# Twelve unread products behind the spread that ends a stage of a two-layer encoder kernel

## The reference

```python
for l in range(DEPTH):                                   # DEPTH = 2
    h = swiglu_ffn(rms_norm(x, ffn1_norm_pre[l]), ffn1_w_in[l], ffn1_w_out[l])
    x = x + 0.5 * rms_norm(h, ffn1_norm_post[l])
    h = rms_norm(x, mix_norm_pre[l]) @ mix_w_in[l]
    ...                                                  # o_gdn and o_cm from h
    h = jnp.concatenate([o_gdn, o_cm], axis=-1) @ mix_w_out[l]
    x = x + rms_norm(h, mix_norm_post[l])
    h = swiglu_ffn(rms_norm(x, ffn2_norm_pre[l]), ffn2_w_in[l], ffn2_w_out[l])
    x = x + 0.5 * rms_norm(h, ffn2_norm_post[l])
    x = rms_norm(x, block_norm[l])
```

## Time and profile before

| | |
|---|---|
| median of 3 runs | 2207.22 us (2206.28 to 2208.68) |
| the profiled execution's own time | 2205.52 us |
| its span | 2203.8 us |
| TensorE products, busy | 2099.9 us, 95% of the span |
| TensorE weight loads, busy | 1756.1 us, 80% |
| VectorE, ScalarE, GpSimd busy | 1239.1, 682.8 and 38.9 us |
| mean granted TensorE clock | 0.967 of full speed |

### The profile page before, as it was taken

The page is one execution under the profiler, slowest core; times in us unless marked ns, Lnnn a source line. Parts: engine busy times, 40 slices in busy tenths (PEclk is TensorE's granted clock), DMA queues, the critical chain, the costliest instruction groups (busy, mean ns, idle before and its releaser), DMA issues.

```text
span 2203.8 us, 26235 instructions
## 1 busy us (share of the span) xinstructions
PE 2099.9 (95%) x10044; PEld 1756.1 (80%) x10044; DVE 1239.1 (56%) x1707; ACT 682.8 (31%) x914; POOL 38.9 (2%) x51
## 2 busy tenths in 40 slices
PE   7999999997988999999999999999979799999997
PEld 6888887875887788888788888878758778888886
DVE  5555422899855755542375554258988656555323
ACT  5222222434225422222242222233341343222222
POOL 0000000000010000000000000000010000000000
PEclk9999999998999999999999999999979999999997
DMA  5333333223001233333233333323220023333320
GB/s 160 104 95 95 98 95 93 77 77 86 1 1 58 77 99 99 97 87 97 84 96 96 95 93 97 97 67 92 81 58 1 1 67 100 99 97 93 96 79 39
DMA packets 345792, 177.54 MB, mean 81 GB/s; under 512 B 8338, under 2 KB 344692, under 8 KB 345716
## 3 DMA queue, kind: packets, MB, share of 16 engines
q1 hardware_dynamic: 344058, 176.34, 28.0%
q10 hardware_dynamic: 1658, 0.16, 0.1%
HBM read 174.38 MB, written 2.10 MB: 80 GB/s over the span
## 4 chain that ended last, share of the span: by engine, by line
PE 77%; DVE 17%; ACT 3%; issue 2%; DMA 0%; DVEq 0%; SPq 0%; ACTq 0%
PE res L457 21%; PE res L459 21%; PE res L458 21%; DVE u L1301 7%; DVE cacc L1385 2%; PE res L521 1%; PE res L522 1%; PE pq L692 1%; PE stat L464 1%; PE res L525 1%; DVE wl L1137 1%; PE bc L485 1%; DVE pre L1371 1%; PE pq L457 1%; PE pq L459 1%
## 5 line engine op out<-in xcount | busy, mean ns | idle before, releaser
L818 ACT ACTIVATE wh<-raw 128x1024 fp32r<-128x1024 f32 (+1 forms) x336 | 347.8, 1037 | 1014.0 <-PE res L459 993.1
L1137 DVE TENSOR_TENSOR wl<-raw,wh 128x1024 fp32r<-128x1024 f32 (+1 forms) x336 | 401.8, 1197 | 392.6 <-ACT wh L818 392.2
L457 PE MATMUL res<-xh,wh 128*128 128x512 f32 x1576 | 614.2, 390 | 3.0 <-DVE xl L1151 3.0
L458 PE MATMUL res<-xl,wh 128*128 128x512 f32 x1576 | 613.2, 389 | 0.0
L459 PE MATMUL res<-xh,wl 128*128 128x512 f32 x1576 | 613.2, 389 | 0.0
L457 PEld LDWEIGHTS res<-xh,wh 128*128 128x128 f32 x1576 | 295.8, 188 | 65.0 <-DVE wl L1137 2.5
L459 PEld LDWEIGHTS res<-xh,wl 128*128 128x128 f32 x1576 | 295.8, 188 | 61.6
L458 PEld LDWEIGHTS res<-xl,wh 128*128 128x128 f32 x1576 | 295.8, 188 | 61.2
L457 PE MATMUL res<-hh,wh 128*128 128x512 f32 x704 | 273.9, 389 | 0.0
L458 PE MATMUL res<-hl,wh 128*128 128x512 f32 x704 | 273.9, 389 | 0.0
L459 PE MATMUL res<-hh,wl 128*128 128x512 f32 x704 | 273.9, 389 | 0.0
(11 more groups left out here) (268 smaller groups left out, 1936.1 us busy)
## 6 DMA issues: line engine op xcount, KB each, us to landing
raw<-in_ffn_w_in SPq DMA_DIRECT2D x176, 512.0 KB, 3.8
raw<-in_ffn_w_out SPq DMA_DIRECT2D x64, 448.0 KB, 3.7
raw<-in_mix_w_in SPq DMA_DIRECT2D x48, 512.0 KB, 4.0
raw<-in_ffn_w_out SPq DMA_DIRECT2D x32, 512.0 KB, 3.8
raw<-in_mix_w_out SPq DMA_DIRECT2D x16, 512.0 KB, 3.9
xin<-in_x SPq DMA_DIRECT2D x4, 512.0 KB, 5.0
out_dram<-xin SPq DMA_DIRECT2D x4, 512.0 KB, 4.0
crows<-in_cm_dw_w ACTq DMA_DIRECT2D x1, 62.0 KB
```

Source lines behind the costliest of these rows:

```text
L457: pe.matmul(bank, wh[:, slot, j, :], hi, start=first, stop=False)
L458: pe.matmul(bank, wh[:, slot, j, :], lo, start=False, stop=False)
L818: act.activation(wh[:, slot, 0:nk, :], raw[:, slot, 0:nk, :], ACT.Copy).then_inc(hi_full, 1)
L1137: dve.tensor_tensor(wl[:, slot, 0:nk, :], raw[:, slot, 0:nk, :], wh[:, slot, 0:nk, :].bitcast(F32), ALU.subtract).then_inc(lo_full, 1)
```

## The change

Behind the spread of the row that ends a stage (q = 1, 3, 5), TensorE does twelve more f32 products of `ident` with `ones`, both 128 x 128, into the first 128 columns of `in_bank(4)`. Nobody reads them; the fifth unit overwrites them. The change is described as "twelve products that nobody reads behind the spread of the row that ends a stage, and the sums of squares of x behind the fourth unit". This is the whole diff:

```diff
@@ -266,6 +266,7 @@
         y_turn, y_first, y_second, s_out = sem("y_turn"), sem("y_first"), sem("y_second"), sem("s_out")
 
+        IDLE_PRODUCTS = 12
         NXR = 3 * KD
         NYQ = 3 * (KD - 2)
 
@@ -492,6 +493,10 @@
                 if q == 1 and l == 0:
                     pe.wait_ge(s_cc, S_CC)
                 spread_column(rmix if q == 2 else rcol).then_inc(bc_full, 1)
+                if q % 2:
+
+                    for n in range(IDLE_PRODUCTS):
+                        pe.matmul(in_bank(4)[:, 0:P], ident[:], ones[:], start=True, stop=True)
 
             def spread_block(l):
 
```

## The result

The changed kernel took 2214.63 us, median of 7 executions (2212.07 to 2220.13), against 2207.66 us (2205.36 to 2211.59) of the kernel before: a ratio of 1.0035, interval 1.0021 to 1.0049, so 7 us slower. That is outside the range given (2205.0 to 2214.5), if by little, and nearest in size to the rival of the long second falls. The traces show that it is not that rival. A second set of 12 executions of the same code gave 2212.46 us (2205.18 to 2218.13), ratio 1.0017 (1.0004 to 1.0030). That median lies inside the range, so on which side of the upper bound the number falls depends on the executions drawn; where the time went does not.

A forecast was written before the change was run, and what follows sets the result against it. TensorE was taken as the bound (77% of the chain). Second falls of 5.6 us less gains of 2.2 gave +3.4 us: 2208.9 for the profiled execution, 2210.6 for the median, range 2205.0 to 2214.5.

The forecast's parts named there:

- the rival of the long second falls: Rival, chance 0.2: half clock behind the sums at stage ends 1, 3 and 4 costs 3.2 us each; +7.4, 2214.6.
- What bounds, and what the products do at a stage end: TensorE bounds; at stage ends 24 records take 2.7 or 5.3 us in a 2.26 us wait and count for the clock.
- What is late next: In the fourth unit, sums of squares cap gains: 1.1 us each at stage ends 1 and 4, 0 at 3.
- The second fall: Clock falls again behind the sums: 1.6 us each at stage ends 1 and 4, 2.4 at 3, sum 5.6.
- What the longer wait does: Lead becomes idling ahead of the sums, about 1.6 us at stage ends 1 and 4, 2.1 at 3; 5.6 us cost.
- The sentence on the Trainium skill's Part 1: Where the clock changes is not tied to the kernel and differs between runs, so no stage-end figure is fixed; no size.
- The rival of the sums moved: Rival, chance 0.05: sums also moved, four waits disappear, 2.4 us arrives at stage ends 1 and 4; up to -5.5, 2201.7.
- products that do not count: Rival, chance 0.08: products do not hold the clock and only delay stage ends 1 to 5; about +5.0 us, 2212.2.

The follow-up runs named there:

- e10: Changed kernel plus filling products inside the mixer, 4 behind the turning of v and 1 ahead of each of four later groups of norms: 2211.59 us, ratio 1.0020.
- e1: The changed kernel run once more, unaltered, for a second profile: 2212.46 us, ratio 1.0017 to the kernel before.
- e9: Kernel before plus the same filling products inside the mixer as e10, none at the stage ends: 2208.21 us, ratio 1.0003.
- e6: Kernel before plus 3 products ahead of the mixer's input spread in both layers, none at the stage ends: 2221.06 us, ratio 1.0064.
- e7: Kernel before plus 15 products ahead of the mixer's input spread in both layers, none at the stage ends: 2213.25 us, ratio 1.0025.
- e2: Changed kernel with the sums of squares of x moved behind the fourth unit in every stage: 2219.29 us, ratio 1.0038.
- e11: As e10, without the products at stage end 3 (q = 5 of the first layer): 2208.62 us, ratio 1.0009.
- e5: Changed kernel with the products at q = 3 and 5 only, none where a mixer follows: 2213.16 us, ratio 1.0024.
- e3: Kernel before with only the sums of squares of x moved behind the fourth unit, no products: 2220.06 us, ratio 1.0049.

## Why the prediction was wrong

- **What bounds, and what the products do at a stage end: right.** The records cost what was given, 2.84 us for 24 at full clock (e10, stage end 4); they count for the clock (half clock in front lasted 3.4 us, or none at all at stage end 1 of e1 and 4 of e10, where it was 6.8 or 10.2 us). The Trainium skill, "TensorE: Matmul & The Clock Gate", Part 4, says that transposes do not bring the full clock. That does not carry over to these products, and the trace disagrees for the turning products too, which the code makes with `pe.transpose`. In the kernel before, TensorE did nothing but 16 of them, of k, for 3.5 us at half clock, and the clock rose (timeline, then slice):

```profile
558.23 3.67 PE L652 MATMUL res<-ident,kT 128*128 128x128 f32 x16 [1.65 <-DVE vb L1428]
```

```profile
561.50:562.00 0.50, 0.45 (x3) 0.09 (x2) 0.35 (x2) 0.50 (x4) 0.00 (x0) 0.75 0.00 0
```

- **What is late next: right at 1 and 3, not at 4.** The waits forecast ahead of the sums were 1.6 us at 1 and 4 and 2.1 at 3; the two profiles of the changed kernel have 1.19 and 1.77 at 1, 2.12 and 1.99 at 3, and 0.34 twice at 4. In e10, where the clock stayed up in front, it was 1.77 at 4. At 1 and 4 the waits stay behind 1.6 where the clock was at half for 3.4 us around the products. Against their spread the sums of these two stage ends started at most 1.2 us earlier than before, near the 1.1 that the prediction gave.
- **The second fall: right as a mechanism.** It came at 1 and 3 in both profiles and not at 4, where the wait stayed at 0.34 us. All stage ends together were forecast at +3.4 us, and measured at +1.05 and +0.06 in the two profiles, too large a forecast by those; with the mixers filled, e10 against e9, it was +3.0 in the profiles. That the medians of e10 and e9 differ by 3.4 us, the forecast's own number, is luck in part: 2.3 us of the profiles' difference lie in a mixer.
- **The step that failed** is in "What the longer wait does": "Behind the sums TensorE runs straight to the spread that all other engines wait for, then through the stage, so this is paid in full". It takes the rest of a stage as a constant that a shift moves along unchanged. The feed-forward rests are (to 0.02 us); the mixers' are not. Added work of 0.7 us at their start costs about 6 us more each in the median (e6, 13.6 less 1.4; in its one profile 1.3 and 8.8), one of 3.4 us nothing beyond itself (e7). In the first profile this term is 12.65 of the 14.6 us, in the second it is 6.3, where the whole difference is 6.2. The prediction had zero for it. The rows were there: the first mixer of before has five stretches at half clock, and I used only as a price list for the stage ends, not as work that the change would move.
- **The rival of the long falls** gave 2214.6, all but the measured median; its number came by luck: no second fall in the two profiles of the changed kernel is longer than 3.4 us. Falls of 6.8 us do occur, in e2, e10 and e11, so it is refuted for the executions profiled and not for every one.
- **The sentence on the Trainium skill's Part 1**, that the place of the clock's changes is not tied to the kernel, was on record as a caveat about the stage ends. It holds, and the executions of one code differ by 13 us; its real weight was in the mixers.
- **The rival of the sums moved** (-5.5 us) was wrong in sign, by the same missing term: e2 gained at stage ends 1 and 4 and lost it all in the mixers.
- **One sum** is off without bearing on this: the parts of the rival "products that do not count" (0.8, 3.2 and 1.4) add up to 5.4 us, not 5.0.

What stays open: why the kernel before is lucky in so many executions. 14 of its 90 executions that came with these runs are at 2211 us or more, which would be one unlucky mixer's worth (none of them was profiled), and none is near 2219. I think that its stretches at half clock ahead of the first units pull the mixer's start to the same position against the clock each time, since work in them ends late by about half of what the rise is late. e5 speaks against this being the whole of it, and no run isolates it. Open too is how the median loss splits: the profiles of the changed kernel put nearly all of it into the mixers, while with the stretch from vb to QK filled 3.4 us are left.

## What to carry to other kernels

A gain at the border of two stages is only worth what the stages behind it keep: check whether their length is the same when they start a microsecond earlier or later, by adding a microsecond of plain work (e6) and then several (e7). If the two answers are not in proportion, then small edits are measured through that effect, and a kernel that has been tuned in place may sit in a lucky position that an edit loses, a harmless one too (e3). Judge such an edit by the clumps of many executions and by stretches of the trace, not by one profile, and fill the sparse stretch itself (e9, e10) before tuning around it.

## What the runs showed of the hardware

- The same instructions of a mixer, from vb to QK, took 17.4, 21.0, 22.3 or 24.8 us, by where the granted clock fell and rose. With the clock rising 4.1 to 4.3 us behind the first vb it stayed up (6 mixers); rising 3.5 to 3.8 us behind it, it fell again 3.4 us later and came back after 10.2 us (8 mixers).
- In the 14 profiles TensorE waited 18 times for 1.1 to 2.4 us ahead of the one-column sums of x at a stage end, and each time the clock went to half within 2.4 us behind the wait. It waited 44 times for 0.3 to 0.6 us, and behind none of these did the clock fall there. Eight such sums and a wait of 1.77 us inside dense work at full clock were followed by 6.8 us at half clock, 1495.24 to 1502.06 (e10), although dense products followed at once.
- Products whose result nobody reads change the clock. 24 records of 128 columns in f32, placed in a wait of 2.26 us, cut the half clock there from 6.8 or 10.2 us to 3.4 us, and at stage end 4 of e10 they kept full clock from there to the wait ahead of the sums.
